# Modulation weights of a four-layer block: 24 slots in each of three mixers, 16 in the fourth, and keys behind them

## What is computed

```
mod = c_act @ w_ada + b_ada            # 1024 x 6144
sh1, sc1, g1, sh2, sc2, g2 = split(mod, 6)
h  = rms_norm(x) * (1 + sc1) + sh1
x  = x + g1 * (mixer(h) @ w_out)
h2 = rms_norm(x) * (1 + sc2) + sh2
x  = x + g2 * ffn(h2)
```

## Time and profile before

| what | value |
|---|---|
| median of 3 runs | 2914.43 us (2911.75 to 2922.51) |
| profiled execution: its own time | 2917.51 us |
| profiled execution: span of the core | 2915.7 us |
| mean granted TensorE clock | 0.923 |
| PE busy | 2421.9 us (83%) |
| DVE busy | 1191.5 us (41%) |
| ACT busy | 585.5 us (20%) |
| POOL busy | 649.2 us (22%) |
| moved by DMA | 934.36 MB, mean 320 GB/s |

### The profile page before, as it was taken

The page is one execution under the profiler, slowest core; times in us unless marked ns, Lnnn a source line. Parts: engine busy times, 40 slices in busy tenths (PEclk is TensorE's granted clock), DMA queues, the critical chain, the costliest instruction groups (busy, mean ns, idle before and its releaser), DMA issues.

```text
span 2915.7 us, 25951 instructions
## 1 busy us (share of the span) xinstructions
PE 2421.9 (83%) x9610; PEld 1279.5 (44%) x9612; DVE 1191.5 (41%) x2851; ACT 585.5 (20%) x1669; POOL 649.2 (22%) x823
## 2 busy tenths in 40 slices
PE   6897987787786987987777786996999988589997
PEld 2466443333332565443333333445454447444543
DVE  1225666667664136567667654023200022330001
ACT  1111332223222021333222222110100012010100
POOL 2102333333332002333333331100122000012200
PEclk8988999999999998999999898997999989799999
DMA  9856999999996656999999996763799113369960
GB/s 382 334 214 250 421 421 422 421 421 422 421 422 280 252 201 255 421 422 421 421 421 421 421 421 286 277 243 130 310 421 421 74 72 116 144 279 421 421 278 15
DMA packets 130077, 934.36 MB, mean 320 GB/s; under 512 B 14240, under 2 KB 16288, under 8 KB 16544
## 3 DMA queue, kind: packets, MB, share of 16 engines
q0 software_dynamic: 114912, 837.01, 69.5%
q1 hardware_dynamic: 15040, 95.70, 8.5%
HBM read 1070.02 MB, written 1.05 MB: 367 GB/s over the span
## 4 chain that ended last, share of the span: by engine, by line
PE 50%; DMA 28%; DVE 15%; ACT 5%; issue 1%; POOL 0%; SPq 0%; DVEq 0%; ACTq 0%
PE units L984 15%; PE units L575 13%; DMA arena<-rows,idx 11%; DMA wide<-rows,idx 10%; PE accs L781 9%; DMA ring<-stream 5%; PE units L962 3%; PE accs L1029 3%; DVE arena L1669 2%; DVE wide L1669 2%; PE accs L634 2%; ACT arena L1192 2%; DMA wide<-ada 2%; PE units L618 1%; DMA wide<-experts 1%
## 5 line engine op out<-in xcount | busy, mean ns | idle before, releaser
L781 PE MATMUL accs<-wide,arena 128*128 128x512 f32 x1036 | 514.0, 651 | 176.0 <-ACT arena L1192 175.8
L781 PE MATMUL accs<-arena 128*128 128x512 f32 x1012 | 482.7, 630 | 99.3 <-ACT arena L1192 99.1
L781 PEld LDWEIGHTS accs<-wide,arena 128*128 128x128 f32 x1036 | 208.9, 207 | 466.4 <-issue 247.2
L575 PE MATMUL units<-arena,ring 128*128 128x256 f32 x1536 | 351.5, 390 | 64.3 <-DVE arena L1856 26.0
L489 POOL DMA_INDIRECT wide<-rows,idx x259 | 244.3, 943 | 604.3 <-PE accs L781 425.8
L984 PE MATMUL units<-wide,arena 128*64 128x512 f32 (+1 forms) x1728 | 369.2, 598 | 9.4 <-DMA wide<-experts 7.7
L781 PEld LDWEIGHTS accs<-arena 128*128 128x128 f32 x1012 | 202.0, 203 | 374.4 <-issue 245.5
L575 PEld LDWEIGHTS units<-arena,ring 128*128 128x128 f32 x1536 | 299.4, 196 | 120.9 <-DVE arena L1375 27.0
L1085 ACT ACTIVATE arena<-units 128x512 f32<-128x512 f32 (+2 forms) x200 | 110.7, 568 | 1110.9 <-PE units L575 466.4
L489 POOL DMA_INDIRECT arena<-rows,idx x253 | 237.8, 940 | 363.8 <-PE accs L781 355.2
L984 PE MATMUL units<-arena 128*64 128x512 f32 (+1 forms) x960 | 232.7, 593 | 0.5 <-ACT arena L1085 0.5
(11 more groups left out here) (298 smaller groups left out, 2027.4 us busy)
## 6 DMA issues: line engine op xcount, KB each, us to landing
wide<-experts POOLq DMA_DIRECT2D x123, 1024.0 KB, 13.4
wide<-experts SPq DMA_DIRECT2D x93, 1024.0 KB
wide<-ada POOLq DMA_DIRECT2D x89, 1024.0 KB, 9.4
ring<-stream SPq DMA_DIRECT2D x70, 1024.0 KB, 6.6
arena<-experts POOLq DMA_DIRECT2D x69, 1024.0 KB, 15.7
arena<-experts SPq DMA_DIRECT2D x51, 1024.0 KB
wide<-ada SPq DMA_DIRECT2D x7, 1024.0 KB, 19.1
wide<-rows,idx POOLq DMA_INDIRECT x259, 21.7
```

The source lines that it names most:

```text
L575: ins = mm(o, a, b, start=start, stop=stop, skip_group_check=True)
L781: ins = mm(o[:, half * 512:(half + 1) * 512], diag[:, i % (2 * GROUP), :], row_slot(PICKS * l + i)[:, D + half * 512:D + (half + 1) * 512] ...
```

## The change

The 24 slots from part 1 of layer l to part 0 of layer l+1 are now read in the mixer of layer l, for l = 0, 1, 2; the RG-LRU mixer reads the last 16. So every layer's parts 1 and 2 are made in its own mixer. In detail:
- SP loads the first eight slots in place of seven; the eighth has room of its own in `arena`. The ring of seven starts behind them, with slot 8.
- POOL at the start: constants, seven ring loads (each behind a read of PE), masks, the other loads up to slot 31, keys. In the later layers its order stays, with other slot numbers, and the RG-LRU mixer gets `ada_loads` too. `expert_loads` waits in both expert layers for the last modulation slot of that layer's mixer.
- Mixer 0 reads 24 slots in the pattern of mixer 1. The RG-LRU mixer reads two behind its eighth projection slot and 14 behind lru_i.
- The columns are made at the beginning of `out_proj`, behind `m_ready`, in layers 0, 1 and 3; in GLA where they were. DVE takes them before the residual. ACT copies the rows at the mixer's end, in the RG-LRU mixer behind its last square root.

The diff, cut (left out: semaphores, the two places of the banks and rows, `take_rows` with its calls, the calls in GLA):

```diff
 ADA_RING = 7
+ADA_FIRST = KT
+ADA_EXTRA_AT = 4096
...
             stage(("mix", l), 0, 1)
-            if l == 0:
-                stage(("mod_rest", l), 0, 1)
...
         if l < DEPTH:
-            stage(("mod", l + 1), 0, 2 if (u + 1) % BANKS == BANKS - 1 else 1)
+            stage(("spare", l), 0, 1 if u % BANKS == BANKS - 1 else 0)
...
-def mod_units(l):
-    u = UNIT_OF["mod", l + 1]
-    if l < DEPTH and UNIT_OF["pq", l] - u == 2:
-        return ((u, 0, 1), (u + 1, 1, ADA_PARTS))
-    return ((u, 0, ADA_PARTS),)
+def pieces(l):
+    return ((l, 1), (l, 2)) + (((l + 1, 0),) if l + 1 < LAYERS else ())
+def before_of(l):
+    return KT + ADA_SLOTS * l
+def after_of(l):
+    return min(KT + ADA_SLOTS * (l + 1), LAYERS * ADA_SLOTS)
...
-            at = i % ADA_RING * SLOT
+            if i == ADA_FIRST - 1:
+                return arena[:, ADA_EXTRA_AT:ADA_EXTRA_AT + SLOT]
+            at = (i if i < ADA_FIRST else i - ADA_FIRST) % ADA_RING * SLOT
...
                 for i in range(first, end):
-                    if i >= ADA_RING:
-                        pool.wait_ge(ada_read, i - ADA_RING + 1)
+                    pool.wait_ge(ada_read, i - (ADA_RING if i >= ADA_FIRST + ADA_RING else ADA_FIRST) + 1)
                     pool.dma_start(ada_piece(i), ada[i]).then_inc(
-                        ada_landed[i % ADA_RING], 16)
+                        ada_landed[(i - ADA_FIRST) % ADA_RING], 16)
...
-                if l == DEPTH:
-                    pool.wait_ge(ada_read, LAYERS * ADA_SLOTS)
+                pool.wait_ge(ada_read, after_of(l))
...
             pool.dma_start(arena[:, 0:FIRST_CONST], first_const[0]).then_inc(const_landed, 16)
+            ada_loads(ADA_FIRST, ADA_FIRST + ADA_RING)
+            first_masks(0)
+            ada_loads(ADA_FIRST + ADA_RING, after_of(0))
             pool.dma_start(keys_sb[:, :, :], keys[0]).then_inc(keys_landed, 16)
-            first_masks(0)
-            ada_loads(ADA_RING, 2 * ADA_SLOTS)
...
                     pool.dma_start(arena[:, 0:GLA_CONST], gla_const).then_inc(const_landed, 16)
-                if l and l + 1 < LAYERS:
-                    ada_loads(ADA_SLOTS * (l + 1), ADA_SLOTS * (l + 1) + ADA_RING)
+                if l:
+                    ada_loads(before_of(l), before_of(l) + ADA_RING)
...
                     first_masks(l)
-                if l and l + 1 < LAYERS:
-                    ada_loads(ADA_SLOTS * (l + 1) + ADA_RING, ADA_SLOTS * (l + 2))
+                if l:
+                    ada_loads(before_of(l) + ADA_RING, after_of(l))
...
-            def mod_cols(u, at, l, first, end):
-                pe.wait_ge(ada_row, ADA_PARTS * l + end)
+            def mod_cols(u, at, which):
+                l, part = which[-1]
+                pe.wait_ge(ada_row, ADA_PARTS * l + part + 1)
                 open_bank(u)
-                for part in range(first, end):
+                for i in range(len(which)):
                     for c in range(4):
-                        row = arena[:, at + (part - first) * 512 + c * P:at + (part - first) * 512 + (c + 1) * P]
-                        ins = mm(bank(u)[:, 16 * part + 4 * c:16 * part + 4 * c + 4], row, ident[:, 0:P:32],
+                        row = arena[:, at + i * 512 + c * P:at + i * 512 + (c + 1) * P]
+                        ins = mm(bank(u)[:, 16 * i + 4 * c:16 * i + 4 * c + 4], row, ident[:, 0:P:32],
...
                 pe.wait_ge(m_ready, l + 1)
+                if l != DEPTH:
+                    mod_cols(UNIT_OF["mods", l], ROWS[l], pieces(l))
...
                 pe.wait_ge(h_ready, 2 * l + 1)
-                each = 1 if l else 2
+                each = 1
...
                     feature_slot(SLOT_OF["conv", l] + s, UNIT_OF["conv", l] + s, hT, adas=each)
-                spread_over = (6, 6, 4, 4, 4) if l == 0 else (4, 3, 3, 3, 3)
+                spread_over = (4, 3, 3, 3, 3)
...
                 ins.then_inc(unit_full[u % BANKS], 1)
-                if l == 0:
-                    mod_cols(UNIT_OF["mod_rest", 0], ROWS_AT, 0, 1, ADA_PARTS)
...
                     token_slots(SLOT_OF["gg", l] + 2 * c, UNIT_OF["gg", l] + 2 * c, hT, adas=2)
-                mod_cols(UNIT_OF["mod", l + 1], ROWS_L2, l + 1, 0, ADA_PARTS)
+                mod_cols(UNIT_OF["mods", l], ROWS[l], pieces(l))
...
                 xc = room(L3["xc"], KT, T)
+                ada_slots(2)
...
                         ins.then_inc(unit_full[(u + blk) % BANKS], 1)
+                ada_slots(2 * KT - 2)
...
                 norm(2 * l + 1)
-                if l < DEPTH:
-                    for u, first, end in mod_units(l):
-                        mod_cols(u, ROWS_AT + first * 512, l + 1, first, end)
...
                 af(room(L3["m"], 2048), room(L3["m"], 2048), ACT.Sqrt).then_inc(m_root, 1)
+                take_rows(ROWS[l], pieces(l))
...
             def next_mods(l):
-                for u, first, end in mod_units(l):
-                    take_mods(u, l + 1, 16 * first, 16 * end)
-                gain_of(0, l + 1, "g1")
-                gain_of(1, l + 1, "g2")
+                take_mods(UNIT_OF["mods", l], pieces(l))
+                gain_of(1, l, "g2")
+                if l + 1 < LAYERS:
+                    gain_of(0, l + 1, "g1")
...
                 wait_taken(dve, u)
-                if l == 0:
-                    take_mods(UNIT_OF["mod_rest", 0], 0, 16, 48)
-                    gain_of(1, 0, "g2")
...
                 (first_mixer if l < DEPTH else gla if l == DEPTH else lru)(l)
+                if l != DEPTH:
+                    next_mods(l)
...
                 norm(2 * l + 1)
-                if l < DEPTH:
-                    next_mods(l)
```

More of the change, by code:

```diff
@@ L101, in plan @@
             stage(("gg", l), 4, 4)
-            stage(("mod", l + 1), 0, 1)
+            stage(("mods", l), 0, 1)
             stage(("decay", l), 0, 2)
@@ L280, in program @@
         slot_read = [sem(f"slot_read{i}") for i in range(RING)]
-        first_landed = [sem(f"first_landed{i}") for i in range(ADA_RING)]
+        first_landed = [sem(f"first_landed{i}") for i in range(ADA_FIRST)]
         ada_landed = [sem(f"ada_landed{i}") for i in range(ADA_RING)]
@@ L380, in ada_piece @@
         def ada_piece(i):
-            at = i % ADA_RING * SLOT
+            if i == ADA_FIRST - 1:
+                return arena[:, ADA_EXTRA_AT:ADA_EXTRA_AT + SLOT]
+            at = (i if i < ADA_FIRST else i - ADA_FIRST) % ADA_RING * SLOT
             return wide[:, at:at + SLOT]
         def ada_bank(l, part):
-            return acc[(part + 3) % 4 if l == 1 else part]
+            return acc[3 if l == 1 and part == 0 else part]
         def row_slot(i):
@@ L409, in _ @@
             sp.dma_start(xT[:, :, :], x.rearrange("(k p) t -> p k t", p=P)).then_inc(x_landed, 16)
-            for i in range(ADA_RING):
+            for i in range(ADA_FIRST):
                 sp.dma_start(ada_piece(i), ada[i]).then_inc(first_landed[i], 16)
@@ L1096, in norm, with take_rows @@
                 af(rstd[:, :], rstd[:, :], ACT.Sqrt).then_inc(std_ready, 1)
-            def take_rows(at, l, first, end):
-                for part in range(first, end):
+            def take_rows(at, which):
+                for i, (l, part) in enumerate(which):
                     act.wait_ge(ada_read, ADA_SLOTS * l + KT * (part + 1))
-                    af(arena[:, at + (part - first) * 512:at + (part - first + 1) * 512], ada_bank(l, part)[:, :],
+                    af(arena[:, at + i * 512:at + (i + 1) * 512], ada_bank(l, part)[:, :],
                        ACT.Copy).then_inc(ada_row, 1)
@@ L1340, in gain_of, with take_mods @@
                 steps.sync()
[L1342 removed]
+            def take_mods(u, which):
                 wait_full(dve, u)
[L1345 to L1347 removed]
+                for i, (l, part) in enumerate(which):
+                    at = COLS["b_ada", l][0] + 16 * part
+                    ins = tt(mods_of[:, l % 2, 16 * part:16 * part + 16], bank(u)[:, 16 * i:16 * i + 16],
+                             cols[:, at:at + 16], ALU.add)
+                    if i < len(which) - 1:
+                        steps(ins)
+                took(ins, u)
                 wait_taken(dve, u)
+                steps.sync()
             def first_mods():
[L1351 removed]
+                take_mods(UNIT_OF["mod", 0], ((0, 0),))
                 gain_of(0, 0, "g1")
             def next_mods(l):
[L1355 to L1358 removed]
+                take_mods(UNIT_OF["mods", l], pieces(l))
+                gain_of(1, l, "g2")
+                if l + 1 < LAYERS:
+                    gain_of(0, l + 1, "g1")
             def norm(i):
```

24 lines of the change are left out of this document (9 added, 15 removed).

## The result

The changed kernel takes 2898.73 us (median, 2893.69 to 2905.07) against 2914.43 for the kernel before in the same comparison: ratio 0.994, 95% interval 0.9919 to 0.9962. The forecast was 2899; the gain is 15.7 us, just over the 14.6 us that the forecast named as what can be told from no change. The profiled execution took 2899.94 us.

What follows compares the result with a forecast made beforehand. PE carried half the chain and DMA 28%, with gather stages at the transfer ceiling and grouped expert stages at full PE. +4.4 - 30.0 + 2.9 + 2.9 + 4.3 = -15.5 us: profiled 2902.0, median 2899; range 2887 to 2911.

Steps and rivals of the forecast that it cites:

- The start: Up to mixer 0's first projection: POOL's ring loads halve SP's rate, slot 7 lands at 40.4; +4.4 us.
- Rival B: At the start: not slowed, POOL's loads flow later or the halves are unequal; 2889 us, chance 0.25.
- Mixer 0: First to output projection: 16 slots leave, 142.1 us becomes mixer 1's 112.15 plus the columns step; -30.0 us.
- The columns: Mixers 0 and 1: the columns step now stands before the output projection and delays it; +2.9 us each.
- I take nothing: Behind the norm in mixers 0 and 1: colder clock after the longer PE gap, ceiling 1.8 us, counted as nothing.
- Mixer 1: Up to its output projection: the columns step in front of it costs +2.9 us.
- RG-LRU: RG-LRU mixer: 16 slots arrive, mostly hidden in the hole; sum +4.3 us (0 to 10).
- lru_i's and the columns' share: RG-LRU mixer: replacement loads cross lru_i's load, +0.5 us (0 to 2.5); 16 of 24 column matmuls, +1.8.
- expert loads' new order: RG-LRU output slots: all 11 expert loads wait for ada_read, so the last out slot is late; +2.0 us (0 to 6).
- some 2 us: RG-LRU hole: last slot copied by 2493, mixer's result at 2495, so the hole covers the slots with this to spare.
- Rival F: RG-LRU mixer: last seven slots read round trip by round trip, +79 us beyond the result; 2978 us, chance 0.03.
- Rival E: RG-LRU hole: POOL's loads flow only while DVE is idle, last slot up to 17.5 us later; 2914, chance 0.05.

Runs made afterwards that it cites:

- start_held: Changed kernel with POOL making the masks first and holding its ring loads until slot 7 has landed; 2892.84 us, 0.9928 of the kernel before.
- before_less16: Kernel before with the 16 slots of layer 1's parts 1 and 2 neither loaded nor read; 2882.74 us, 0.9876.
- experts_held: Changed kernel with expert loads of layers 2 and 3 held until the last output slot has landed; 2886.28 us, 0.9897 of the kernel before.
- lru_none: Changed kernel without the RG-LRU mixer's 16 slots, expert loads in the order of the kernel before; 2903.33 us, 0.9955 of the kernel before.
- changed_again: The changed kernel itself, unedited, run once more beside the kernel before; 2897.56 us, 0.995.

## Why the prediction was right

The total hit; the terms did less well, and part of the hit is luck. By the traces the sum was off by 1.3 at the start, by 1.7 behind mixer 0, by -3.4 in mixer 1 and by -1.6 in stretches that it did not forecast, which nearly cancels: -15.5 forecast, -17.6 measured, and -15.7 in the medians.

**The start: +4.4 forecast, +5.7 measured; mechanism right.** Slot 7 was read at 40.91 for 40.4. POOL issued at 14.62 and not at 15.65, as PE read slot 0 earlier than assumed (13.21), but the half rate began only 4.5 us later and not 4.2. The rest is the columns step of the start, which ran 1.87 us where `start_held` shows it at 1.05: 7.8 us from slot 7 to the projection in place of 1.94 + 5.03. Rival B (2889) is out; the halves are equal.

**Mixer 0: -30.0 + 2.9 = -27.1 forecast, -27.2 measured;** the step was right, the closeness is luck. Taking mixer 1 as the measure of mixer 0, in place of PE's 14.9 us, carried the forecast, and `before_less16` confirms it with -30.5. But the two mixers differ by more than the slots. Mixer 1 of the kernel before held a late ring slot and matmuls at the low clock,

```profile
975.96 8.80 PE L575 MATMUL units<-ring,arena 128*128 128x512 f32 x16 [2.27 <-DMA ring<-stream]
```

together some 5.5 us that the changed mixer 0 doesn't have; and that mixer keeps a stage of attention at 10.34 us, 5.47 in mixer 1, together with its neighbours 5.4 us. The two cancel. The same code of mixer 0 took 109.7, 114.9, 115.1 and 116.8 us in the traces of `experts_held`, the changed kernel, `lru_none` and `changed_again`.

**The columns: +2.9 per mixer forecast.** The step took that, 2.81 and 0.17 more idle time in front. Wrong was "I take nothing" for a colder clock: the output projection rose from 27.89 to 29.56, +1.67 in both mixers of this trace, close to the ceiling of 1.8 that the forecast named for the first slot behind the norm. It falls in front of the residual instead. In mixer 1 the norm then ran 1.6 faster than in mixer 0 (3.69 against 5.29), so that its output stage came out even.

**Mixer 1: +2.9 forecast, -0.5 measured.** Its 2.27 us wait for a ring slot, and the projection slot behind it, which ran 8.80 for 7.1 at low clock, had no counterpart afterwards (0.31). That is phase and not the edit: the counts are the same in both kernels, and `before_less16`, whose mixer 1 is that of the kernel before, has no wait for the ring there.

**RG-LRU: +4.3 forecast, +4.6 measured.** lru_i's and the columns' share came as 0.9 for the late row copy and 1.8 for the step, and the four output slots took 38.6 for 36.65, +1.9, where +2.0 stood. But `lru_none` and `before_less16`, both with the old pattern of loads, take 38.6 and 38.7 as well, so the runs don't lay that term on the expert loads' new order: it lies within what this place varies, and that it came out is luck. The margin of "some 2 us" was none, -0.9: PE waited 3.51 us for the third of the last seven slots, which landed 5.4 us behind the second, and ACT's copy counts as well. Rival F needed only that margin to be passed, and was still no danger: seven loads in flight make the excess a slot's length and not a round trip.

**Rival E, the port:** in the hole the last five slots were read at 2456.87, 2459.36 and so on to 2466.76, one per 2.48 us, with DVE busy 17.45 of 26 us. The first of the five came some 3 us late, but the transfers did not stop for it: POOL issued the five together at 2447.76, and in every 2 us from 2447 to 2463 the DMA engines were busy 0.93 or more. The Trainium skill says in "SBUF — State Buffer", section "SBUF: two separate sides", that POOL's descriptors have to wait while DVE runs an operation in its two-port mode. No effect of that is seen here, and no run shows which of these operations, if any, run in that mode: that rule was not put to the test.

**Not forecast:** GLA -5.7, the stretch after it -2.2, the last stretch +4.4 and the second gather +1.9, together -1.6, in code that the change hardly touches. In GLA it can be read: the norm-to-columns time fell from 134.9 to 132.1, mostly because a ring slot that had been 2.18 us late was followed by 1.67 us of low clock, which no late slot was afterwards (the waits themselves add up to 3.9 before and 3.3 after), and the steps and output slots behind it gained as much again (the first product behind the columns took 3.34 before and 1.96 after). In the last stretch the norm took 5.38 for 3.69, and the 32 matmuls ahead of the first expert 6.66 for 5.16: clock again. Why the clock fell out so is open; no run here was made for it.

## What to carry to other kernels

The price of moved work is not its busy time: 16 slots with 14.9 us of matmuls cost 26 to 30 us where PE and the transfers were busy (89% and 0.82) and 0.9 us in a hole of 26 us. The first could be read from a stage that does the same work without them, to within the 5 us that such a stage varies by itself. A prefetch released early took half of the rate from what was wanted now; let it wait for the landing of the last urgent transfer, if its own reader is far away. Keep a chain of very narrow matmuls out of the path in front of a long projection, and sum it with what the clock does behind it.

## What was not expected of the hardware

The granted clock fell to 0.50 while PE was busy throughout, behind 24 matmuls with four moving columns (2.8 us): the windows above. The Trainium skill, "TensorE: Matmul & The Clock Gate", section "HAM oscillation — how this bites in real kernels", tells of clock lost to waits for transfers. In this place there was none: the share of the DMA engines was 0.00 until 165 us and PE's only wait 0.76 us for DVE, the same with the doubled chain, which was still running when the clock fell and kept it low three times as long. So waits for transfers are not the only cause.

One and the same stage, 48 matmuls of the weighted sum in attention, takes 5.5 to 10.3 us from mixer to mixer and kernel to kernel, by the clock alone. In the changed kernel, PE, mixers 0 and 1, and in `experts_held`, whose code is the same up to mixer 0's end, mixer 0:

```profile
141.79 10.34 PE L752 MATMUL units<-arena 128*128 128x64 f32 x48
...
1021.45 5.47 PE L752 MATMUL units<-arena 128*128 128x64 f32 x48
```

```profile
141.86 5.47 PE L754 MATMUL units<-arena 128*128 128x64 f32 x48
```

So a single trace carries some 5 us per mixer that belong to no edit. That is a third of the gain forecast here, and why the small terms were judged by stretches and the whole by medians.
